# Moving the base blocks of 64x64 triangular inverses with two 256-column products in place of eight of 64 columns

## The chip, the cores and the metric

The kernel runs on one core of a Trainium2 chip. The metric is the device time of one execution in microseconds (us). TensorE is the matrix engine: PE stands for its products, PEld for its weight loads. VectorE is DVE, ScalarE is ACT, GpSimd is POOL.

## What is computed

Two transformer blocks, one behind the other, on 256 tokens of width 1024. The second one mixes tokens with two recurrences, a gated delta rule (GDN) and an RWKV-7 scan, both in chunks of 64 tokens and in two directions. Each chunk and head needs the solution of a unit lower triangular system of size 64. The kernel forms the inverse of that matrix; what is computed, cut to the part that matters, is

```python
CHUNK = 64
H_A, H_B = 4, 8                       # heads of GDN, of RWKV

def gated_delta_chunked(q, k, v, g, beta, s0):
    ...
    lower = jnp.where(strict, jnp.einsum('...id,...jd->...ij', k_beta, k) * decay, 0.0)
    a_mat = jnp.eye(CHUNK, dtype=jnp.float32) + lower
    rhs = jnp.concatenate([v * beta[..., None], k_beta * jnp.exp(gc)[..., None]], axis=-1)
    sol = lax.linalg.triangular_solve(a_mat, rhs, left_side=True, lower=True, unit_diagonal=True)
    ...

def rwkv7_scan(r, w, k, v, a, b, s0):
    def step(s, inp):
        r_t, w_t, k_t, v_t, a_t, b_t = inp
        sa = jnp.einsum('...vk,...k->...v', s, a_t)
        s = s * w_t[..., None, :] + sa[..., :, None] * b_t[..., None, :] + v_t[..., :, None] * k_t[..., None, :]
        return s, jnp.einsum('...vk,...k->...v', s, r_t)
    ...
```

The RWKV scan is computed in chunks of 64 too, so each of its chunks needs such an inverse as well.

## The kernel before

Each engine has its own in-order instruction stream; engines wait for each other on semaphores (`wait_ge`, `then_inc`). Up to about 1598 us the first block and the projections run. The GDN scan follows (about 1598 to 1712 us), then projections for RWKV, the RWKV scan (about 1830 to 2100 us), and the experts.

`Inverse64` (L1637) inverts eight 64x64 matrices at once. They lie as four blocks `c` side by side, in partitions 0 to 63 and again in 64 to 127; `HALVES` (L1622) gives for each half its own partitions and the other half's. The inverse is built by doubling: a base with blocks of size 2, then five levels. `TX[:, 0]` holds the inverse in one half order, `TX[:, 1]` its transpose in the other.

The base has four steps. POOL masks the matrices (`base_pool`, L1656), DVE adds the identity and so makes `Mb` (`base_dve`, L1662), PE moves it (`base_pe`, L1667), ACT copies both results from PSUM to SBUF (`base_act`, L1677, its instructions at L1682). `base_pe` fills two PSUM banks. `ps` gets each block transposed, in its own half: `Mb` is the stationary operand and the identity streams. `pt` gets each block as it is, in the other half: the identity is stationary and `Mb` streams. All of it goes through `mm` (L282). The mark `turned` follows the last product, and ACT waits for it before both copies.

The 64x64 products use a quarter of TensorE's array each. I call the quarters by rows and columns: A (rows 0 to 63, columns 0 to 63), B (rows 0 to 63, columns 64 to 127), C (rows 64 to 127, columns 0 to 63), D (rows 64 to 127, columns 64 to 127). A product reads its own half's partitions (its rows) and writes the partitions of its columns. So `ps` uses A and D, `pt` uses B and C, and the code before goes round A, B, D, C.

`mid_pe` (L1690) is the first product of a level and uses B and C; its right operand for level 1 is the ACT copy `inv_0`. `level_pe` (L1707) is the second product and uses all four quarters, except on the last level of RWKV.

The order of work is written by hand. `gdn_order` (L1738) lists pieces for four rounds, in each of which `base_b` runs `base_pe` for two inverses one behind the other. `rwkv_order` does the same for eight rounds. That makes 12 places with `base_pe` twice, 24 inverses, and 384 products of 64 columns. The list decides what PE does right behind them: in RWKV the piece `prep 0`, a 64x128 product and a one-row product of 512 columns each, and then `mid` of level 1; in GDN, by round, the `z` projection, `mid`, or products of the state.

An f32 product is issued as two weight loads and two products, and each of the two shows in the trace as a record of its own. So a 64-column f32 product is four instructions in PE's stream.

Of the kernel before, what the change touches and what calls it, by code (L numbers as in the profile page):

```python
# [32 lines left out]
C_I64, C_P64, C_Q64, C_L64 = 2690, 2754, 3010, 3138  # L33
# [54 lines left out]
class Counts:  # L88
# [13 lines left out]
    def did(self, name, *key, by=1):  # L102
        count = SHARED.get(name, name)
        self.n[count] = self.n.get(count, 0) + by
        self.value[(name, *key)] = self.n[count]
        return self.sem(name), by

    def at(self, name, *key):
        return self.sem(name), self.known[(name, *key)] if self.known else 1
# [112 lines left out]
def program(nc, A, out, known):  # L222
    stack = ExitStack()
    with stack:
# [22 lines left out]
        def bank(product, *readers, among=every_bank):  # L247

            n = bank_at.get(among, 0)
            b = among[n % len(among)]  # L250
            bank_at[among] = n + 1
            for mark in bank_free[b]:
                PE.wait_ge(*at(*mark))
            bank_free[b] = readers
            bank_of[product] = b
            return PS[b]
# [13 lines left out]
        def cst(col, n=128):  # L270
            return CST[:, col:col + n]
# [9 lines left out]
        def mm(o, lhsT, rhs, start, stop):  # L281
            return M.matmul(o, lhsT, rhs, start=start, stop=stop, skip_group_check=True)  # L282
# [1339 lines left out]
        HALVES = ((slice(0, 64), slice(64, 128)), (slice(64, 128), slice(0, 64)))  # L1622
# [14 lines left out]
        class Inverse64:  # L1637
# [29 lines left out]
            def base_pe(self, banks):  # L1667
                ps = bank(("turned", *self.tag), ("inv_own", *self.tag), among=banks)
                pt = bank(("turned_t", *self.tag), ("inv_0", *self.tag), among=banks)
                PE.wait_ge(*at("inv_t", *self.tag, 0))  # L1670
                for c in range(4):
                    for own, other in HALVES:
                        mm(ps[own, 64 * c:64 * c + 64], self.Mb[own, c, :], cst(C_I64, 64)[own, :], True, True)
                        ins = mm(pt[other, 64 * c:64 * c + 64], cst(C_I64, 64)[own, :], self.Mb[own, c, :], True, True)
                ins.then_inc(*did("turned", *self.tag))

            def base_act(self):  # L1677
# [2203 lines left out]
```

## Time and profile before

| | us |
|---|---|
| median of 3 runs | 2506.0 |
| lowest, highest | 2505.88, 2506.99 |
| the profiled execution | 2505.72 |
| its span in the trace | 2504.3 |

| engine | busy us | share of the span |
|---|---|---|
| PE | 2413.2 | 96% |
| PEld | 2085.4 | 83% |
| DVE | 1409.3 | 56% |
| ACT | 1193.5 | 48% |
| POOL | 294.3 | 12% |

PE's busy time counts any instant at which at least one product is under way. The sum over products that run beside each other in different quarters is larger. The granted clock was 0.993 of full speed on average.

### The profile page before, as it was taken

Reading aid. Unit: us, or ns where it says so; the run is one execution under the profiler, and the core shown is the slowest. Engines: PE = TensorE matmul, PEld = TensorE weight load, DVE = VectorE, ACT = ScalarE, POOL = GpSimd, SP = SyncE. Lnnn points to the kernel's source line nnn. Section 1 sums busy time; section 2 is a strip of 40 time slices with the busy share of each in tenths; the row PEclk is TensorE's granted clock in tenths of the full one; section 3 lists DMA queues with packets and bytes.
Section 4 is the critical chain, followed back from the end, with each engine's and each line's share of the span. In section 5 each row is a group of like instructions: output and inputs, shape, how many; then the busy total and the mean of one; then the engine's idle time right before and its main releaser. Section 6 shows DMA issues by size and latency. Waiting matters only on the chain.

```text
span 2504.3 us, 52401 instructions
## 1 busy us (share of the span) xinstructions
PE 2413.2 (96%) x23215; PEld 2085.4 (83%) x23215; DVE 1409.3 (56%) x2208; ACT 1193.5 (48%) x1725; POOL 294.3 (12%) x417
## 2 busy tenths in 40 slices
PE   7999999999999999999999999999999888999998
PEld 7999888799999998878899995687477777778787
DVE  5655544376646655533566557453534554378886
ACT  5434465544444434475454436431244442277775
POOL 0100000031101100000211000372123322000000
PEclk9999999999999999999999999999999999999999
DMA  8764522366656654413367522201111011479995
GB/s 256 244 211 152 203 83 92 116 202 202 227 194 202 216 203 160 167 70 119 127 204 255 194 97 101 69 4 40 68 36 37 24 50 41 134 250 365 368 362 183
DMA packets 269445, 396.15 MB, mean 158 GB/s; under 512 B 9624, under 2 KB 173133, under 8 KB 269085
## 3 DMA queue, kind: packets, MB, share of 16 engines
q1 hardware_dynamic: 267481, 389.32, 45.6%
q8 instruction: 185, 3.03, 0.5%
q0 software_dynamic: 1120, 2.17, 0.3%
q10 hardware_dynamic: 612, 1.24, 0.1%
q14 instruction: 47, 0.39, 0.1%
HBM read 391.66 MB, written 1.05 MB: 157 GB/s over the span
## 4 chain that ended last, share of the span: by engine, by line
PE 83%; DVE 6%; DMA 5%; ACT 3%; issue 2%; POOL 0%; SPq 0%; ACTq 0%; DVEq 0%; POOLq 0%
PE ps L282 82%; DMA RB<-in_moe_w_up 5%; DVE gwl L447 2%; ACT gwh L438 1%; DVE wl L447 0%; PE ps L1146 0%; ACT wh L438 0%; DVE AR L657 0%; ACT AR L2898 0%; DVE AT L1231 0%; DVE AR L1967 0%; PE ps L541 0%; ACT AR L2890 0%; ACT AT L1200 0%; DMA VR<-in_diff_gain 0%
## 5 line engine op out<-in xcount | busy, mean ns | idle before, releaser
L447 DVE TENSOR_TENSOR wl<-RB,wh 128x2048 fp32r<-128x2048 f32 (+5 forms) x189 | 412.5, 2186 | 284.8 <-ACT wh L438 284.3
L282 PE MATMUL ps<-H,RB 128*128 128x256 f32 (+2 forms) x1728 | 452.8, 421 | 2.8 <-ACT AR L2869 1.3
L438 ACT ACTIVATE wh<-RB 128x2048 fp32r<-128x2048 f32 (+5 forms) x189 | 342.2, 1815 | 232.6 <-PE ps L282 203.1
L282 PEld LDWEIGHTS ps<-H,RB 128*128 128x128 f32 (+1 forms) x1728 | 320.2, 189 | 114.9 <-issue 77.0
L282 PE MATMUL ps<-xhf,wl 128*128 128x256 f32 x1408 | 403.0, 286 | 3.7 <-DVE xlf L686 3.7
L282 PE MATMUL ps<-xlf,wh 128*128 128x256 f32 x1408 | 399.5, 284 | 0.0
L282 PE MATMUL ps<-xhf,wh 128*128 128x256 f32 x1408 | 399.4, 284 | 0.0
L282 PE MATMUL ps<-AR 64*64 64x64 f32 (+3 forms) x8296 | 258.3, 231 | 40.9 <-issue 24.0
L282 PEld LDWEIGHTS ps<-AR 64*64 64x64 f32 (+2 forms) x8296 | 225.1, 138 | 79.3 <-issue 64.3
L282 PEld LDWEIGHTS ps<-xhf,wl 128*128 128x128 f32 x1408 | 271.3, 193 | 14.2 <-issue 10.1
L282 PEld LDWEIGHTS ps<-xlf,wh 128*128 128x128 f32 x1408 | 271.4, 193 | 0.1
L282 PEld LDWEIGHTS ps<-xhf,wh 128*128 128x128 f32 x1408 | 271.3, 193 | 0.0
L447 DVE TENSOR_TENSOR gwl<-RB,gwh 128x2048 fp32r<-128x2048 f32 x96 | 217.2, 2289 | 37.2 <-ACT gwh L438 35.6
L438 ACT ACTIVATE gwh<-RB 128x2048 fp32r<-128x2048 f32 x96 | 183.2, 1926 | 44.2 <-DMA RB<-in_moe_w_up 30.1
L282 PE MATMUL ps<-hh,wl 128*128 128x256 f32 x704 | 199.2, 283 | 0.0
L282 PE MATMUL ps<-hl,wh 128*128 128x256 f32 x704 | 199.2, 283 | 0.0
L282 PE MATMUL ps<-hh,wh 128*128 128x256 f32 x704 | 199.2, 283 | 0.0
L791 ACT ACTIVATE H<-H 128x256 f32<-128x256 f32 x88 | 36.9, 419 | 294.7 <-DVE H L827 294.7
L282 PEld LDWEIGHTS ps<-hh,wl 128*128 128x128 f32 x704 | 135.2, 192 | 0.0
L282 PEld LDWEIGHTS ps<-hl,wh 128*128 128x128 f32 x704 | 135.2, 192 | 0.0
L282 PEld LDWEIGHTS ps<-hh,wh 128*128 128x128 f32 x704 | 135.2, 192 | 0.0
L1467 POOL TENSOR_TENSOR H<-H 128x256 f32<-128x256 f32 x48 | 45.6, 986 | 685.7 <-DVE H L1438 685.7
(445 smaller groups left out, 4105.3 us busy)
## 6 DMA issues: line engine op xcount, KB each, us to landing
RB<-in_ffn_w_gu SPq DMA_DIRECT2D x88, 1024.0 KB, 7.8
RB<-in_w_in SPq DMA_DIRECT2D x23, 2048.0 KB, 7.7
RB<-in_ffn_w_down SPq DMA_DIRECT2D x16, 2048.0 KB, 7.8
RB<-in_w_gate SPq DMA_DIRECT2D x16, 2048.0 KB, 8.7
RB<-in_moe_w_gate SPq DMA_DIRECT2D x32, 1024.0 KB, 7.6
RB<-in_moe_w_up SPq DMA_DIRECT2D x32, 1024.0 KB, 10.2
RB<-in_moe_w_down SPq DMA_DIRECT2D x32, 1024.0 KB, 8.0
RB<-in_ada_w SPq DMA_DIRECT2D x12, 2048.0 KB, 9.9
```

The source lines that it names most:

```text
L282: return M.matmul(o, lhsT, rhs, start=start, stop=stop, skip_group_check=True)
L438: S.activation(self.pair(h)[0], of(slot_of(*key)), ACT.Copy).then_inc(*did("high", *mark))
L447: V.tensor_tensor(lo, of(slot_of(*key)), hi.bitcast(F32), ALU.subtract).then_inc(*did("low", *mark))
L791: S.activation(sil[:, n % 4, 0, :], sil[:, n % 4, 0, :], ACT.Silu).then_inc(*did("silu", f, n))
L1467: P.tensor_tensor(HB[:, c, :], HB[:, c, :], tmp[:, (8 * i + c) % 4, :], ALU.add).then_inc(*did("merged", l, br, c))
```

## The change

In `base_pe` the loop over `c` now issues the products for `ps` alone, eight of 64 columns. Behind it come two products for `pt`, one for each half, that stream all four blocks (256 columns) through the identity. The mark `turned` is still on the last product. The values are the same.

```diff
                 for c in range(4):
-                    for own, other in HALVES:
+                    for own, _ in HALVES:
                         mm(ps[own, 64 * c:64 * c + 64], self.Mb[own, c, :], cst(C_I64, 64)[own, :], True, True)
-                        ins = mm(pt[other, 64 * c:64 * c + 64], cst(C_I64, 64)[own, :], self.Mb[own, c, :], True, True)
+
+                for own, other in HALVES:
+                    ins = mm(pt[other, 0:256].rearrange("p (c n) -> p c n", c=4), cst(C_I64, 64)[own, :], self.Mb[own],
+                             True, True)
                 ins.then_inc(*did("turned", *self.tag))
```

On PE, at the first place in the GDN scan (round 0): `ps<-CST,AR` is a product for `ps` (the constants stream), `ps<-AR,CST` one for `pt`. The rows ahead belong to the value rows, `ps<-RB,H` behind is the `z` projection.

```order
 L282 MATMUL ps<-RB,H 64x256 x32
 L282 MATMUL ps<-CST,AR_14745 64x128 x16
-L282 MATMUL ps<-CST,AR_14745 64x64
-L282 MATMUL ps<-AR_14745,CST 64x64
...
+L282 MATMUL ps<-CST,AR_14745 64x64 x8
+L282 MATMUL ps<-AR_14745,CST 64x256 x2
+L282 MATMUL ps<-CST,AR_14745 64x64 x8
+L282 MATMUL ps<-AR_14745,CST 64x256 x2
 L282 MATMUL ps<-RB,H 64x256 x16
```

What were 32 alternating products for the two inverses are now 8, 2, 8 and 2. Nothing else moved.

At the second place on PE (round 1 of GDN) the products of `mid`, which use B and C, stand right behind:

```order
 L282 MATMUL ps<-CST,AR_14745 64x64 x8
 L282 MATMUL ps<-AR_14745 64x64 x72
-L282 MATMUL ps<-CST,AR_14745 64x64
-L282 MATMUL ps<-AR_14745,CST 64x64
...
+L282 MATMUL ps<-AR_14745,CST 64x256 x2
+L282 MATMUL ps<-CST,AR_14745 64x64 x8
+L282 MATMUL ps<-AR_14745,CST 64x256 x2
 L282 MATMUL ps<-AR_14745 64x64 x16
```

There the last product for `pt` now stands next to `mid`, in the same quarters. DVE, ACT, POOL and SP keep their instructions and order.

## Rows read from the trace of the kernel before

**Rows 1.** The page's chain that ended last, shares of the span

```profile
PE 83%; DVE 6%; DMA 5%; ACT 3%; issue 2%; POOL 0%; SPq 0%; ACTq 0%; DVEq 0%; POOLq 0%
```

**Rows 2.** Chain of one RWKV round, 1860 to 1905: start, us, what

```profile
1859.99 1.88 PE ps L282 x82
1861.87 1.41 issue
1863.28 13.56 PE ps L282 x302
...
1880.15 7.17 PE ps L282 x253
1887.33 0.50 issue
1887.83 1.03 PE ps L282 x38
1888.87 0.12 issue
1888.99 1.97 PE ps L282 x85
1890.95 1.32 issue
1892.27 3.24 PE ps L282 x122
1895.51 0.50 issue
1896.01 9.00 PE ps L282 x144
```

**Rows 3.** PE groups by form, 1598 to 2110: busy us, mean ns, idle before, releaser

```profile
L282 PE MATMUL ps<-AR,CST 64*64 64x64 f32 x384 | 14.5, 222 | 0.0
```

**Rows 4.** Timeline of one place, RWKV round 1: start, us, what, xcount [idle before]

```profile
1870.00 0.27 PE L282 MATMUL ps<-CST,AR 64*64 64x64 f32 x1
...
1870.10 0.22 PE L282 MATMUL ps<-CST,AR 64*64 64x64 f32 x1
...
1870.16 0.22 PE L282 MATMUL ps<-CST,AR 64*64 64x64 f32 x1
...
1870.76 1.21 ACT L1682 ACTIVATE AR<-ps 128x256 f32<-128x256 f32 x4 [0.27 <-PE ps L282]
...
1870.92 0.22 PE L282 MATMUL ps<-CST,AR 64*64 64x64 f32 x1
1870.93 0.22 PE L282 MATMUL ps<-AR,CST 64*64 64x64 f32 x1
1870.93 0.22 PE L282 MATMUL ps<-CST,AR 64*64 64x64 f32 x1
1870.94 0.22 PE L282 MATMUL ps<-AR,CST 64*64 64x64 f32 x1
...
1871.09 1.12 PE L282 MATMUL ps<-H,AR 64*128 64x512 f32 x2
...
1872.14 1.12 PE L282 MATMUL ps<-H,CST 1*128 1x512 f32 x2
```

**Rows 5.** Timeline, a 256-column f32 product in two column halves at once

```profile
1604.14 1.90 PE L282 MATMUL ps<-RB,H 128*64 128x256 f32 x16
```

**Rows 6.** PE groups by form under way in 1958.30 to 1958.33

```profile
L282 PE MATMUL ps<-AR 64*64 64x64 f32 x9 | 0.5, 219 | 0.0
```

**Rows 7.** The same, 1958.335 to 1958.345, then 1958.56 to 1958.58

```profile
L282 PE MATMUL ps<-AR 64*64 64x64 f32 x8 | 0.4, 218 | 0.0
L282 PE MATMUL ps<-AR 64*64 64x128 f32 x2 | 0.3, 320 | 0.0
...
L282 PE MATMUL ps<-AR 64*64 64x128 f32 x4 | 0.4, 294 | 0.0
L282 PE MATMUL ps<-AR 64*64 64x64 f32 x6 | 0.3, 218 | 0.0
```

**Rows 8.** Timeline of GDN round 1, where the second inverse comes later

```profile
1629.66 0.27 PE L282 MATMUL ps<-CST,AR 64*64 64x64 f32 x1 [0.95 <-DVE AR L1664]
...
1630.14 0.22 PE L282 MATMUL ps<-AR,CST 64*64 64x64 f32 x1
1630.42 0.66 ACT L1682 ACTIVATE AR<-ps 128x256 f32<-128x256 f32 x2 [2.54 <-PE ps L282]
1630.50 0.24 PE L282 MATMUL ps<-CST,AR 64*64 64x64 f32 x1
...
1630.98 0.22 PE L282 MATMUL ps<-AR,CST 64*64 64x64 f32 x1
1631.18 1.12 PE L282 MATMUL ps<-AR 64*64 64x64 f32 x20
1631.26 0.66 ACT L1682 ACTIVATE AR<-ps 128x256 f32<-128x256 f32 x2 [0.17 <-PE ps L282]
```

**Rows 9.** Who PE waited for, 1598 to 2110: us in total, times, longest

```profile
PE ps L282 <- issue: 25.6, 24, 2.8
PE ps L282 <- POOL AR L1687: 5.8, 3, 2.2
PE ps L282 <- DVE AR L1664: 2.8, 4, 1.0
```

**Rows 10.** PE's timeline around three stalls of one round

```profile
2056.72 0.81 PE L282 MATMUL ps<-AR 64*64 64x64 f32 x40 [1.12 <-issue]
...
2060.69 2.14 PE L282 MATMUL ps<-AR 64*64 64x64 f32 x128 [0.92 <-issue]
2064.60 0.62 PE L282 MATMUL ps<-AR 64*64 64x64 f32 x25 [1.77 <-issue]
```

**Rows 11.** DMA queues of instructions: whole span, then 2060.68 to 2064.3 alone

```profile
q8 instruction: 185, 3.03, 0.5%
...
q8 instruction: 1, 0.02, 1.6%
```

**Rows 12.** Timeline of RWKV round 7, where `mid` follows the base directly

```profile
2074.69 0.22 PE L282 MATMUL ps<-AR,CST 64*64 64x64 f32 x1
2075.27 0.45 PE L282 MATMUL ps<-AR 64*64 64x64 f32 x14 [0.36 <-ACT AR L1682]
```

**Rows 13.** The scans' stretch: us, then busy us (x instructions) of each engine

```profile
1601.00:2110.00 509.00, 460.93 (x10570) 365.78 (x10566) 233.22 (x532) 186.45 (x446) 174.40 (x262) 0.99 0.12 37
```

## The prediction

> **What bounds the kernel.** I read the chain that ended last first: PE holds 83% of it, and no other engine more than 6% [rows 1]. In the scans, where the change lies, the chain is PE's own products, broken by pieces named "issue", in which PE waited for nothing that the profile shows [rows 2]. The waits of PE between 1598 and 2110 us say the same in sum: 25.6 us went to "issue" in 24 stalls, 5.8 us to POOL's masks and 2.8 us to the DVE step just ahead of the base [rows 9]. So time on PE counts nearly in full here, and there are two currencies: how long the array's quarters are held, and how many instructions PE's stream holds. The change costs in the first and saves in the second.
>
> The products that it removes are few. The 384 records for `pt` had PE busy 14.5 us in total [rows 3], and that time is not what can be gained, since nearly all of it lies beside the products for `ps`.
>
> **How the base runs now.** In RWKV round 1 the first record starts at 1870.00, the next ones at 1870.10 and 1870.16, the last four at 1870.92 to 1870.94 [rows 4]. Two inverses are 32 products, so 64 records, and these come as 16 groups of four, one record in each quarter. From 1870.10 to 1870.92 there are 14 steps in 0.82 us: 0.058 us a step. All quarters are free one step behind the last start, at 1870.98, so a place takes 0.98 us. The four quarters are full. The four products of `pt` in B are hidden behind the four of `ps` in A, and C behind D.
>
> **What a product of 256 columns takes.** The trace has none in a quarter of the array. The nearest is the `z` projection, 256 columns in two column halves at once: 16 records in 1.90 us, in eight steps, the last of which runs 0.38 us: (1.90 - 0.38) / 7 = 0.217 us a step [rows 5]. That is four times 0.058 less a small fixed part. A quarter with one such product is held 2 x 0.216 = 0.43 us. Before, four products of 64 columns held it 8 x 0.058 = 0.47 us. The bounds are 0.43 and, if a small fixed part came with each block, 0.47. I take 0.43. So B and C have no more work than before, and the question is only when they start it.
>
> **When B and C start.** Now eight products for A and D are issued first. In the last level of RWKV round 3, products of 64 columns are in B and C; behind them in the stream stand products of 128 columns for A and D. Up to 1958.33 records of 64 columns alone are under way [rows 6]; by 1958.345 two of 128 columns are under way too, and at 1958.56 six of 64 columns are, each lasting 0.22 us, so started after 1958.34 [rows 7]. Older narrow products thus start behind the first wide ones, three in each of their two quarters, with one just started in each. So a free quarter doesn't wait for the others to finish: its work starts when the busy ones have four records each left, and different widths run beside each other. I take that as the rule of this kernel's stream: each quarter holds two products, four records.
>
> The Trainium skill ("TensorE: Matmul & The Clock Gate", What overlaps and what doesn't) says that matmuls start and end strictly in program order. The rows above show later products starting ahead of older ones, so the measurement decides against that; what that rule would cost is the first rival below.
>
> **The sum for two inverses one behind the other.** Count from the first start. A and D run 16 steps as before and are free at 0.98. They have four records left of the first inverse when step 5 starts, at 0.10 + 3 x 0.058 = 0.27. B and C then start: 0.05 more for the first record of an idle quarter (0.10 against 0.058 between the first two starts, [rows 4]) and 0.43, so they are free at 0.75. The second inverse's A and D records have gone on meanwhile. Four are left at step 13, at 0.10 + 11 x 0.058 = 0.74; B and C go on at 0.75 and are free at 1.19. That is 0.21 us later than 0.98. Nine of the 12 places are of this kind (GDN rounds 0 and 2, RWKV rounds 1 to 7): 9 x 0.21 = 1.9 us.
>
> **For inverses that come apart.** In GDN round 1 the first runs from 1629.66 to 1630.14 and the second from 1630.50, because it waits for DVE [rows 8]; GDN round 3 and RWKV round 0 look the same. There the first is covered by the wait. The second took 0.10 + 7 x 0.058 = 0.51 us and takes 0.75: 0.24 later. Three places: 0.7 us.
>
> **Who feels it.** In RWKV rounds 0 to 6 the next product is of another tile shape, 64 rows by the full width. It starts at 1871.09, 0.15 us behind the last record's start [rows 4], so it waits for all quarters and starts later by what B and C take. ACT's copies start at 1870.76 and take 1.21 us, to 1871.97 [rows 4]. The first copy may start some 0.25 us later, which keeps the end at about 1872.2, and `mid` starts only behind the second 512-column product that began at 1872.14 and took 1.12 us: that delay is hidden. It would cost as soon as the copies ended more than 1 us later. In GDN round 1 and RWKV round 7 `mid` waits for these copies [rows 8, 12], so there the delay of `turned` is on the path, and it is the same 0.2 to 0.25 us, not another one. In GDN rounds 0, 2 and 3 other products follow and PE's end moves as in RWKV. Nothing runs free behind: the later waits for POOL and DVE hang on PE's own products. In all 1.9 + 0.7 = **2.6 us of cost**. From below the cost is bounded by nothing, if B and C start at the front of the stream in a way that no row shows; from above by the first rival.
>
> **What the shorter stream gives back.** The change removes six products for each inverse, 24 instructions, so 576 in all. The stalls on "issue" come in a rhythm: 2056.72, 2060.69, 2064.60 [rows 10]. Between the last two PE started 128 records, which with their weight loads are 256 instructions, and the queue that brings instructions moved one packet; over the span it moved 185 in 3.03 MB, 16 KB each, 256 instructions of 64 bytes [rows 10, 11]. So PE's stream comes in lines of 256, and where PE uses one up in less than some 3.9 us it waits for the next. The Trainium skill ("Advanced Engine Details and Errata", ISA Cache) says lines of 256 instructions too; the rows give the time. 576 instructions are 2.25 lines. Spread over all lines of the scans (10570 records and 10566 weight loads between 1601 and 2110 us, [rows 13], so 83 lines) the 25.6 us are 0.3 us a line and 2.25 lines give 0.7 us. If each saved line is one that stalls (24 stalls, 1.07 us each) they give 2.4 us. The base itself lies between long products, where lines don't stall, but its going shifts every later line end, in steps of 48 instructions a place, into other parts of the rounds. I take the middle, **1.5 us of gain**, and give the shift 3 us either way.
>
> **Sum.** 2.6 - 1.5 = +1.1 us against the profiled execution's 2505.7 us, which lies 0.3 us under the median of 2506.0. I put the difference on the median: 2507.1 us. What a measurement of this kernel can tell from no change is about 0.2%, 5 us.
>
> **Rivals.**
> 1. *The quarters don't overlap (slower).* If B and C start only behind the last record of A and D, and the next inverse's A and D only behind them, each inverse takes 8 x 0.058 + 0.43 us in place of 0.47. 24 x 0.43 = 10.4 us, less 1.5: +8.9, 2514.9 us. The skill's strict order would give nearly this. Against it stand [rows 6, 7]. It decides where the overlap of a wide and a narrow product falls under half of each. Chance 8%.
> 2. *The line ends fall badly (slower).* The 24 stalls last up to 2.8 us [rows 9]. If the shift adds five average stalls, 5 x 1.07 = 5.4 us, in place of the saving, the kernel takes 2.6 + 5.4 = +8.0, 2514.0 us. For it speaks that every round behind the first place gets other line ends; against it that there are fewer lines. Chance 6%.
> 3. *The stream is the bound (faster).* If lines, and not quarters, pace all of the scans, the wider products cost nothing and 2.25 lines of 3.9 us each are saved (from 2060.69 to 2064.60, [rows 10]): -8.8, 2497.2 us. Half of it, -4.4, would already show the base as covered. Against it: the base stands behind long products, and no stall is at its place in [rows 4]. Chance 6%.
>
> **How the numbers follow.** The forecast has 80%, with its own range of 2503 to 2511 us: the shift of 3 us either way, and 1 us for the cost. The whole range should leave out no more than 2 in 10; it reaches into the slower rivals, which hold more than the faster one: 2503 to 2513 us. Faster by over 0.2% (under 2501): part of rival 3 and a tail, 5%. Slower by over 0.2% (over 2511): rivals 1 and 2 and a tail, 14%. Within 0.2%: 81%.
>
> **What would show it in the trace after.** At each place 32 records of 64 columns and 8 of 256, the latter of about 0.38 us each and 0.216 us apart in one quarter. The first wide records start about 0.3 us behind the first narrow one, while narrow ones go on; if they start at 0.5 us, rival 1 holds. `prep 0` starts 1.3 us behind the base's first record, not 1.09. ACT's first copy starts about 0.25 us later. The stalls on "issue" stay about 24, at other places, with a sum of 21 to 28 us, and the instruction queue moves two or three packets fewer. I am wrong if the scans' stretch grows or shrinks by more than 4 us while those records look as I say, for then the stalls or a wait that I didn't see carry it.

## The result, and the profile after

The changed kernel takes **2512.97 us** (median of 20 runs, 2506.68 to 2516.46); the kernel before, timed in turn with it on the same chip, takes 2508.78 us (20 runs, 2503.91 to 2513.47). The ratio is **1.0019 (1.0013 to 1.0024)**. A second set of runs on another chip gave 1.0020 (1.0011 to 1.0029). So the change costs 4.8 us (0.5 us of standard error over both sets; means against means), where +1.1 us was forecast. That is still inside the 0.2% called "no change", and the time of 2512.97 us is inside the range, at its upper end. But the cost is certain, and it is four times the forecast. The profiled execution took 2510.31 us.

Who PE waited for from 1598 to 2115 us (us in total, times, longest), beside [rows 9]:

```profile
PE ps L282 <- issue: 26.3, 25, 2.6
PE ps L282 <- POOL AR L1690: 4.6, 3, 2.2
PE ps L282 <- DVE AR L1664: 2.4, 3, 1.1
```

The records of the 48 wide products, in PE's groups by form (busy us, mean ns, idle before), and the queue that brings instructions (packets, MB, share):

```profile
L282 PE MATMUL ps<-AR,CST 64*64 64x256 f32 x96 | 13.8, 398 | 0.0
...
q8 instruction: 183, 3.00, 0.5%
```

The 384 records of [rows 3] have become 96, nearly as busy as before (13.8 us against 14.5). Two packets fewer have come than in [rows 11], as forecast, but the stalls on "issue" did not shrink: 26.3 us in 25 against 25.6 in 24 (the prediction had 21 to 28 us in about 24).

The place of [rows 4], RWKV round 1, in the timeline after (start, us, engine, what, xcount, idle before):

```profile
1871.60 0.51 PE L282 MATMUL ps<-CST,AR 64*64 64x64 f32 x10
...
1871.89 0.43 PE L282 MATMUL ps<-AR,CST 64*64 64x256 f32 x2
1871.93 0.40 PE L282 MATMUL ps<-CST,AR 64*64 64x64 f32 x8
...
1872.16 0.38 PE L282 MATMUL ps<-AR,CST 64*64 64x256 f32 x2
...
1872.59 1.21 ACT L1685 ACTIVATE AR<-ps 128x256 f32<-128x256 f32 x4 [0.50 <-PE ps L282]
1872.62 0.38 PE L282 MATMUL ps<-AR,CST 64*64 64x256 f32 x2
...
1872.93 1.12 PE L282 MATMUL ps<-H,AR 64*128 64x512 f32 x2
```

Read it beside [rows 4]. The narrow records start at 1871.60 and the first wide ones 0.29 us behind, while narrow ones go on beside them. `prep 0` starts 1.34 us behind the first record where it started 1.09 us behind, so the place takes 0.25 us more. ACT's first copy starts 0.99 us behind the first record, before 0.76. All contiguous places but the one in RWKV round 7, where PE waits for ACT, show the same 1.34 us.

The next rows show something that the prediction had left out altogether. They are windows of RWKV round 1 after (us, then busy us and instructions of PE, PEld, DVE, ACT, POOL; the third figure from the end is the granted clock, 0.50 being 1.2 GHz):

```profile
1893.00:1894.00 1.00, 0.31 (x23) 0.17 (x11) 0.78 (x3) 0.00 (x0) 0.00 (x0) 1.00 0.00 0
1894.00:1895.00 1.00, 0.00 (x0) 0.00 (x0) 0.00 (x0) 0.00 (x0) 0.00 (x0) 1.00 0.00 0
1895.00:1896.00 1.00, 0.85 (x24) 0.85 (x28) 0.00 (x0) 0.38 (x1) 0.00 (x0) 0.65 0.00 0
1896.00:1897.00 1.00, 1.00 (x31) 1.00 (x29) 0.45 (x2) 0.00 (x0) 0.00 (x0) 0.50 0.07 16
...
1898.00:1899.00 1.00, 1.00 (x29) 1.00 (x28) 0.42 (x1) 0.98 (x2) 0.00 (x0) 0.64 0.00 0
1899.00:1900.00 1.00, 1.00 (x42) 1.00 (x39) 0.81 (x2) 0.56 (x1) 0.35 (x1) 1.00 0.00 0
```

The chain of the same stretch (start, us, what) tells what lies ahead of it:

```profile
1889.27 0.92 issue
...
1891.11 2.20 PE ps L282 x101
1893.31 1.84 issue
1895.15 4.86 PE ps L282 x120
```

PE waited 1.84 us for its stream. It went on at 1895.15, and 0.15 us later the clock fell to 1.2 GHz and stayed there for 3.4 us. At half speed 3.4 us do the work of 1.7. The same round before had its stalls of 1.32 and 0.50 us at other products ([rows 2], from 1890.95 on) and kept its clock at 1.00. The trace before has three such stretches in the scans (near 1620, 1651 and 1712 us), the trace after has three of the same kind (near 1626, 1653 and 1714 us) and the one above.

The stall does not decide this by itself. A second trace of the same changed kernel has the same stall at the same product, and no fall of the clock behind it (chain, then window):

```profile
1894.59 2.20 PE ps L282 x101
1896.79 1.56 issue
1898.35 5.70 PE ps L282 x154
...
1898.35:1904.05 5.70, 5.70 (x159) 5.50 (x160) 4.15 (x11) 2.43 (x4) 1.69 (x3) 1.00 0.02 6
```

So a stall can be followed by a slow stretch that costs as much again, but it need not be. Over the whole execution the clock does not tell the two profiled executions apart either: it is 0.993 in both, and they lie 4.6 us apart. From the start of the first place to that of the last the scans took 5.0 us longer after (477.4 against 472.4); 2.8 of that is in the eleven places between, and the one more stretch at 1.2 GHz is worth 1.7.

### The profile page after: what moved, and what is told of

It reads as the page before. It is cut to its first block, busy times and chain, and to the rows that moved or that the text cites. A ratio compares the mean times of both kernels' runs of the same rounds, so it can differ in the third digit from the quotient of the medians.

```text
span 2508.9 us, 51825 instructions
## 1 busy us (share of the span) xinstructions
PE 2419.5 (96%) x22927; PEld 2088.0 (83%) x22927; DVE 1409.3 (56%) x2208; ACT 1193.8 (48%) x1725; POOL 296.0 (12%) x417
## 4 chain that ended last, share of the span: by engine, by line
PE 82%; DVE 6%; DMA 5%; ACT 4%; issue 2%; POOL 0%; SPq 0%; ACTq 0%; DVEq 0%; POOLq 0%
PE ps L282 81%; DMA RB<-in_moe_w_up 4%; DVE gwl L447 2%; ACT gwh L438 1%; DMA RB<-in_moe_w_down 0%; DVE wl L447 0%; PE ps L1146 0%; ACT wh L438 0%; DVE AR L657 0%; ACT AR L2901 0%; DVE AT L1231 0%; DVE AR L1970 0%; PE ps L541 0%; ACT AR L2893 0%; ACT AT L1200 0%
```

## The experiments

None of the kernels leaves work out. "Mean" below is the mean of a kernel's runs less the mean of the runs of before in the same set, with one standard error, worked out from the single runs. "Clock" is the mean granted clock of the same runs, less before's. Over 2506 us, 0.001 of it is 2.5 us of TensorE's full-speed work lost, which is an upper figure for the time it costs, since a slower TensorE waits less for its stream. Each figure in that column has a standard error of 0.0003 to 0.0008, so most of them are not clear of nothing one by one.

| kernel | place, us | ratio (95%) | mean, us | clock |
|---|---|---|---|---|
| changed | 1.34 | 1.0019 (1.0013 to 1.0024) | +4.3 ± 0.8 | |
| changed, again | 1.34 | 1.0020 (1.0011 to 1.0029) | +5.4 ± 0.8 | -0.0006 |
| two loops, all of 64 columns | 1.49 | 1.0015 (1.0006 to 1.0024) | +3.6 ± 1.1 | -0.0002 |
| wide first | 1.09 | 1.0000 (0.9991 to 1.0009) | -0.2 ± 0.9 | -0.0009 |
| wide first, again | 1.09 | 1.0002 (0.9993 to 1.0011) | +0.9 ± 0.9 | -0.0012 |
| wide after two | 1.08 | 1.0000 (0.9991 to 1.0009) | 0.0 ± 0.7 | -0.0015 |
| wide first twice | 1.87 | 1.0016 (1.0006 to 1.0026) | +4.0 ± 0.9 | -0.0004 |
| GDN alone, wide first | 1.09 | 1.0007 (0.9998 to 1.0016) | +1.8 ± 1.0 | -0.0016 |
| GDN alone, as changed | 1.34 | 1.0018 (1.0008 to 1.0028) | +4.7 ± 1.2 | -0.0022 |
| RWKV alone, wide first | 1.09 | 0.9992 (0.9983 to 1.0001) | -2.0 ± 0.8 | +0.0003 |
| RWKV alone, wide first, again | 1.09 | 0.9995 (0.9983 to 1.0008) | -1.0 ± 1.3 | -0.0013 |
| RWKV alone, as changed | 1.34 | 1.0000 (0.9990 to 1.0011) | -0.4 ± 1.0 | +0.0004 |
| before, 64 wait instructions ahead | 1.09 | 1.0005 (0.9996 to 1.0014) | +1.3 ± 0.9 | -0.0007 |
| changed, filled with waits | 1.34 | 1.0150 (1.0136 to 1.0164) | +37.6 ± 0.7 | -0.0068 |

"Place" is a contiguous place, from its first product to the next other one.

**The order alone, in a stream of the old length.**

```diff
                 for c in range(4):
-                    for own, other in HALVES:
+                    for own, _ in HALVES:
                         mm(ps[own, 64 * c:64 * c + 64], self.Mb[own, c, :], cst(C_I64, 64)[own, :], True, True)
+                for c in range(4):
+                    for own, other in HALVES:
                         ins = mm(pt[other, 64 * c:64 * c + 64], cst(C_I64, 64)[own, :], self.Mb[own, c, :], True, True)
```

> The kernel before with the order of the change alone: the eight products for ps first, then the eight products of 64 columns for pt. Same instructions in number and length, so the stream's line ends stay where they were. Theory Q (the order costs: B and C start only once A and D have four records left, 0.27 us after the first start): a contiguous place is then 0.27 + 4 x 0.23 = 1.19 us in place of 0.98, +0.2 us at each of 12 places, +2.4 us in all, a ratio of 1.0010 (1.0006 to 1.0014). Rival S (the quarters cost nothing, and all that the change moved is where line ends fall): same as before, 1.0000 within 0.0004.

Slower by 3.6 us, with not one instruction more or less. The order costs, and rival S (only line ends count) falls. RWKV round 1 in its timeline:

```profile
1867.62 0.51 PE L282 MATMUL ps<-CST,AR 64*64 64x64 f32 x10
1867.92 0.27 PE L282 MATMUL ps<-AR,CST 64*64 64x64 f32 x2
...
1869.12 0.69 PE L282 MATMUL ps<-H,AR 64*128 64x512 f32 x1
```

B and C start 0.30 us behind A and D, as in the changed kernel. The place grew by 0.40 us, not 0.2. My working for it had forgotten that the stream is one. The likely reason for the rest is that the second inverse's products for A and D stand behind the later products of `pt` while these wait for room in B and C. The twelve places of this trace add up to 4.5 us more than before's, and 3.6 ± 1.1 were measured.

**The wide pair first.**

```diff
+                for own, other in HALVES:
+                    mm(pt[other, 0:256].rearrange("p (c n) -> p c n", c=4), cst(C_I64, 64)[own, :], self.Mb[own],
+                       True, True)
                 for c in range(4):
                     for own, _ in HALVES:
-                        mm(ps[own, 64 * c:64 * c + 64], self.Mb[own, c, :], cst(C_I64, 64)[own, :], True, True)
-
-                for own, other in HALVES:
-                    ins = mm(pt[other, 0:256].rearrange("p (c n) -> p c n", c=4), cst(C_I64, 64)[own, :], self.Mb[own],
-                             True, True)
+                        ins = mm(ps[own, 64 * c:64 * c + 64], self.Mb[own, c, :], cst(C_I64, 64)[own, :], True, True)
```

> The changed kernel with the two wide products ahead of the eight narrow ones. The stream is as short as the changed kernel's. Theory Q: all four quarters start at once (pt's two wide ones of 0.43 us lie in B and C while A and D take their four narrow ones of 0.22 us), so the place is 0.98 us again or a little less and the 3.0 us that the order cost are back; what is left over before is the shift of the line ends, +0.9 to +1.7 us: a ratio of 1.0003 to 1.0007, and about 3 us under the changed kernel. Rival S: no different from the changed kernel, 1.0019 (1.0013 to 1.0024).

> The kernel with the two wide products ahead of the eight narrow ones once more, word for word, beside the changed kernel. Theory Q (the order is what costs, 0.25 us at each of 12 places): 3.0 us under the changed kernel; the two measured so far stand 4.9 us apart, 1.3 us of uncertainty, over different chips. Theory G (the shorter stream is worth the 1.5 us of the prediction's sum): 0.9994 of before. Rival C (what the shorter stream gives in stalls is taken back by the granted clock: the first trace has six stretches at 1.2 GHz in the scans in place of three, each 3.4 us long and so worth 1.7 us): 1.0000 of before within 0.0004, with the mean clock 0.001 lower than before's.

Beside it, on the chip of the second set, ran the changed kernel:

> The changed kernel once more, word for word, beside its variants on one chip, so that they can be set against it directly; its trace tells whether the four stretches of 3.4 us at a granted clock of 1.2 GHz that the first trace has in the scans (at 1623, 1653, 1713 and 1893 us) belong to the program or to one execution. Theory Q: 1.0010 to 1.0024 of before, as measured before. Theory P (the stretches belong to the program): the same four places again; rival: others.

RWKV round 1 with the wide pair first:

```profile
1869.73 0.43 PE L282 MATMUL ps<-AR,CST 64*64 64x256 f32 x2
1869.74 0.45 PE L282 MATMUL ps<-CST,AR 64*64 64x64 f32 x8
...
1870.56 1.21 ACT L1684 ACTIVATE AR<-ps 128x256 f32<-128x256 f32 x4 [0.34 <-PE ps L282]
...
1870.82 1.12 PE L282 MATMUL ps<-H,AR 64*128 64x512 f32 x2
```

Wide and narrow start together, and the place is 1.09 us as in the kernel before. On one chip it stood 4.5 us (± 1.0) under the changed kernel, with the same number of instructions: theory Q holds in sign, and its 3.0 us lie 1.5 standard errors off. Theory G had 0.9994 for the shorter stream; 1.0000 and 1.0002 came. Each of the two intervals still holds 0.9994; all three sets of kernels with short places and the short stream together (+0.2 ± 0.5 us, next experiment) do not, and with them theory G falls. The clock was lower by 0.0009 ± 0.0005 and 0.0012 ± 0.0004, as rival C had it. The traces' stretches at 1.2 GHz belong partly to the program: both wide-first traces have one near 1620 or 1625 us and others near 1653, 1680, 1824 and 1841, and one more each, at 1997 and at 2026. The changed kernel's second trace, which runs 3 to 4 us later there, has those near 1629, 1657 and 1718 again, but not the one at 1895 shown above; it has two others, near 1684 and 2001.

**The wide pair behind two narrow products.**

```diff
                 for c in range(4):
                     for own, _ in HALVES:
-                        mm(ps[own, 64 * c:64 * c + 64], self.Mb[own, c, :], cst(C_I64, 64)[own, :], True, True)
+                        ins = mm(ps[own, 64 * c:64 * c + 64], self.Mb[own, c, :], cst(C_I64, 64)[own, :], True, True)
+                    for own, other in HALVES if c == 0 else ():
+                        mm(pt[other, 0:256].rearrange("p (c n) -> p c n", c=4), cst(C_I64, 64)[own, :], self.Mb[own],
+                           True, True)
```

> The two wide products behind the first two narrow ones, the other six narrow ones last: between the changed kernel (wide behind eight narrow ones) and wide-first. A look at the trace. Theory H (what costs is the head: narrow products ahead of the first wide one, during which pt's two quarters stand empty, and a wide one takes TensorE for 0.25 us wherever it lies): from a contiguous place's first product to the next other product 1.09 us plus 0.04 to 0.06 us, so 1.13 to 1.15 us; the changed kernel has 1.34. Rival (any narrow product ahead costs as much as all eight, since the start of both quarters is what counts): 1.3 us or more.

> The kernel with the wide pair behind the first two narrow products, word for word as looked at, now timed. Its places are 1.08 us in the trace, 0.26 us under the changed kernel's, with the same stream as wide-first. Theory Q: as wide-first, 1.0000 to 1.0003 of before, 3 to 4.5 us under the changed kernel. Rival (it was not the place but something else of wide-first that gained): 1.0010 or more.

The trace of the single execution of the first run:

```profile
1870.60 0.27 PE L282 MATMUL ps<-CST,AR 64*64 64x64 f32 x2
1870.62 0.43 PE L282 MATMUL ps<-AR,CST 64*64 64x256 f32 x2
1870.71 0.34 PE L282 MATMUL ps<-CST,AR 64*64 64x64 f32 x6
...
1871.68 0.69 PE L282 MATMUL ps<-H,AR 64*128 64x512 f32 x1
```

1.08 us from the first product to the next other one. Theory H (a narrow product ahead costs its own step, 1.13 to 1.15) and its rival both miss. One narrow product each in A and D leaves room, so the wide ones start 0.02 us behind. With four each in front they start 0.29 us behind. That fits the prediction's rule: two products, four records, for each quarter. Timed, it equals wide first. Over the three sets of kernels with short places and the short stream the mean is +0.2 ± 0.5 us; the changed kernel stands 4.6 ± 0.7 above them.

**The wide pair twice.**

```diff
-                for own, other in HALVES:
+                for own, other in 2 * HALVES:
                     mm(pt[other, 0:256].rearrange("p (c n) -> p c n", c=4), cst(C_I64, 64)[own, :], self.Mb[own],
```

> Wide-first with each pair of wide products issued twice (the second pair writes the same values again), 192 instructions more in the scans. Theory W (a wide product takes TensorE for 0.25 us even where its quarter is another than the last one's): a contiguous place grows from 1.09 to 2.1 us, each of the 12 places by 1.0 us, and if a place's time is paid one for one, 12 us over wide-first: 1.0048 of before. Rival Q2 (quarters work side by side, 0.43 us for a pair of wide ones): 1.73 us for the place, +0.64 each, 7.7 us: 1.0031. Rival X (a place's time is paid more than one for one, as 4.5 us for 12 x 0.25 us suggest): 18 us, 1.0072.

```profile
1871.99 0.43 PE L282 MATMUL ps<-AR,CST 64*64 64x256 f32 x2
...
1872.26 0.38 PE L282 MATMUL ps<-AR,CST 64*64 64x256 f32 x2
...
1873.33 0.38 PE L282 MATMUL ps<-AR,CST 64*64 64x256 f32 x2
...
1873.55 0.38 PE L282 MATMUL ps<-AR,CST 64*64 64x256 f32 x2
1873.86 1.12 PE L282 MATMUL ps<-H,AR 64*128 64x512 f32 x2
```

The wide records come two at a time, one in B and one in C, 0.22 us apart. Eight such steps from 1871.99 end at about 1873.75, 1.76 us: the quarters work side by side. Theory W would have 2.1 us. So the 0.43 us that the prediction gave a pair is right; my W had taken the starts' distance for the price of one product. The contiguous places grew by 0.78 us each (the others, which begin with a wait, by 0.4), 8.2 us over all 12, and the time by 3.8 ± 1.0 us over wide first (4.0 less 0.2). So a place's time is not paid one for one, and rival X falls too. One would think that the stream catches up while the array is held longer, but the trace does not show it: PE's stalls on "issue" in the scans are 25.3 us in 24, against 25.6 and 22.2 us in the two traces of wide first. Why only half is paid stays open.

**Each scan alone.** The new base applies only where a test of the inverse's tag holds ("r" for the RWKV scan, "g" for the GDN scan), and the other scan keeps the base of before:

```diff
+                if self.tag[0] == "r":
...
+                else:
                     for c in range(4):
                         for own, other in HALVES:
...
```

> The kernel before with wide-first bases in the four GDN places alone; the eight RWKV places keep the sixteen narrow products, so the RWKV scan's code is before's and only its line ends fall 192 instructions earlier. Theory G: 192 instructions are 0.75 of a line, worth -0.5 us; theory L (where line ends fall matters more than how many there are): off 1 by 1 us or more, in either direction; nothing at all: 1.0000 within 0.0004.

> The kernel before with wide-first bases in the eight RWKV places alone, where TensorE waits for its instruction stream most (23.5 of 26 us in the scans). The GDN scan is before's to the instruction. Theory G: 384 instructions fewer there are 1.5 lines, worth -1.0 us (-0.5 to -1.6): 0.9996; rival C: 1.0000 with a lower mean clock; rival L: 1 us or more in either direction by the line ends.

> The kernel with wide-first bases in the RWKV scan alone, word for word, a second time: at 0.9992 (0.9983 to 1.0001) it was the fastest so far, and its interval still held 1. Theory G (a shorter stream in the scan that waits for it is worth 1.5 to 2 us): 0.9992 to 0.9996 again, with a pooled interval under 1. Rival (chance): 1.0000 or above.

> The change in the RWKV scan alone (narrow ones first, then the wide pair), GDN as before. Its twin in the stream, wide-first in RWKV alone, stood at -1.7 us (0.7 us of uncertainty, two runs). Theory Q (0.25 us at each place, paid one for one): 8 x 0.25 = 2.0 us above the twin, so +0.3 us: 1.0001 of before. Rival X (paid at one and a half): 3.0 us above, +1.3 us: 1.0005. Rival R (the RWKV scan is where the whole changed kernel loses): +4.8 us, 1.0019.

> The change in the GDN scan alone, RWKV as before. Its twin, wide-first in GDN alone, stood at +1.8 us (1.0 us of uncertainty). Theory Q: 4 x 0.25 = 1.0 us above the twin, +2.8 us: 1.0011. Rival X: 1.5 us above, +3.3 us: 1.0013. Rival T (the twin's +1.8 was chance, and the GDN places cost their 1.0 us alone): 1.0004.

The order costs +1.2 ± 1.2 us in the eight RWKV places (-0.4 against the -1.7 ± 0.7 pooled of wide first there) and +2.9 ± 1.5 in the four GDN places. Expected were 2.0 and 1.0. Both lie within 1.3 standard errors, so these runs don't show more than 0.25 us a place. The shorter stream with short places gives **-1.7 ± 0.7 us** in RWKV alone, near the 1.0 that theory G asked for (its two runs gave -2.0 ± 0.8 and, repeated, -1.0 ± 1.3), and **+1.8 ± 1.0** in GDN alone. Together they are nothing, as wide first in both scans is; but of the four kernels' intervals here only that of the change in GDN alone leaves out 1. The change as it stands loses nothing in RWKV alone (1.0000) and shows its loss in GDN alone (1.0018). PE's stalls on "issue" from 1598 us to the scans' end, first in the trace with GDN alone changed, then in that with RWKV alone:

```profile
PE ps L282 <- issue: 25.4, 26, 2.6
```

```profile
PE ps L282 <- issue: 23.1, 21, 2.8
```

The windows of the two scans in the same order:

```profile
1598.00:2120.00 522.00, 476.55 (x10566) 377.80 (x10561) 235.31 (x538) 188.63 (x448) 176.71 (x266) 0.97 0.11 36
```

```profile
1598.00:2110.00 512.00, 467.58 (x10451) 369.41 (x10446) 234.68 (x535) 187.77 (x447) 175.29 (x264) 0.99 0.12 37
```

A granted clock of 0.97 against 0.99 over some 515 us is about 10 us of work lost, though this execution was one of the slower ones of its kernel (2513.7 us at a median of 2509.6). Over all runs the mean clock was 0.0022 ± 0.0006 lower than before's with GDN changed, and 0.0004 ± 0.0004 higher with RWKV changed. The table leans the same way: in the nine sets whose line ends in the RWKV scan are moved from its first place on, the clock was lower by 0.0004 to 0.0068; in the four where they start that scan as before, it differs by +0.0004, +0.0003, -0.0002 and -0.0013.

Where line ends fall does not fix it, though. In the two kernels with GDN alone changed (wide first, then as changed) the RWKV scan has before's code, and its line ends fall alike, since both save the same 192 instructions. From its first place to its last:

```profile
1839.90:2075.30 235.40, 213.45 (x6096) 183.21 (x6096) 113.52 (x267) 108.75 (x256) 73.90 (x101) 0.99 0.10 30
...
1840.60:2083.50 242.90, 218.79 (x6096) 186.51 (x6096) 113.58 (x267) 108.76 (x256) 73.56 (x101) 0.96 0.10 29
```

The same 6096 records took 235.4 us in one execution and 242.9 in the other, with 6.8 and 17.1 us at 1.2 GHz (5.1 us of work apart) and 13.9 and 17.9 us of stalls on "issue". So single executions differ by more here than any effect that is looked for, and that moved line ends bring the clock down is a lean of the means, not shown.

**Moving the line ends alone.**

```diff
+        def pad(n):
+            for _ in range(2 * n):
+                PE.engine.wait_ge(*at("x_in", 6))
...
             def conv_pe():
                 for n in range(13):
+                    if n in (1, 2):
+                        pad(32)
```

> The kernel before with 64 satisfied waits in TensorE's stream ahead of the GDN scan (32 in each of two convolution steps), so that every line end in both scans falls 64 instructions earlier in the work; nothing else differs. It tells how much the position of line ends is worth alone. Theory L (the sum's shift term was too small, the stalls at line ends differ by microseconds): moves by 1 us or more in either direction, a ratio off 1 by over 0.0004. Rival (the shift averages out over the 12 rounds): within 0.7 us, 0.9997 to 1.0003.

+1.3 ± 0.9: between the two theories, and undecided. `pad(n)` asks for 2n waits, and they come out as n instructions with two waits each: TensorE's queue has 636 wait instructions in this trace and 572 in before's. The waits are not free. They run from 1500.4 to 1507.2 us, one every 0.106 us, and where PE had no work left it stood still for 2.72 us; the clock fell behind that stall too, to 0.57 in the mean of 1504 to 1508 us. The first base starts 1.6 us later than before and the last one 0.5 us later. So in this one execution the scans took 1.1 us less, which is well inside what executions differ by. The trace shows how stalls and clock can trade: the stalls on "issue" in the scans fell from 25.6 us to

```profile
PE ps L282 <- issue: 19.0, 16, 2.5
```

and yet its span is 2505.4 us against 2504.3. It has eight stretches at 1.2 GHz in the scans, against three. The RWKV scan before, and with the line ends moved:

```profile
1837.27:2111.06 273.79, 240.52 (x7116) 206.43 (x7116) 123.09 (x293) 118.28 (x282) 86.88 (x125) 1.00 0.10 28
```

```profile
1838.00:2112.00 274.00, 245.13 (x7116) 212.27 (x7116) 123.45 (x293) 118.42 (x282) 87.45 (x125) 0.98 0.10 28
```

The same 7116 records, 274 us both times, 4.6 us more of them busy and less waited: the clock 0.02 lower took what the stalls gave. This is one pair of traces.

**The changed kernel, its stream filled up again.**

```diff
                     mm(ps[:, :], TW[u.rr, u.ts], W2[u.rr, :], True, False)
+                    if i > 0:
+                        pad(24)
```

(and the same behind the second product of `prep 0`, and four times `pad(48)` in the projections ahead of the RWKV scan)

> The changed kernel with waits that are already satisfied put into TensorE's stream so that, in the RWKV scan, line ends fall at the same products as in the kernel before: 48 in each of the eight RWKV rounds (24 between the two products of prep 0 and 24 behind them), and 480 over four steps of the projections ahead of that scan, of which 192 would make up for the GDN scan; the base is the changed one. Theory Q (order costs 0.25 us at each of 12 places): slower than before by 3 us plus what the waits themselves take, a ratio of 1.0012 or more. Rival S (line ends alone): with its line ends back in the RWKV scan it stands within 1 us of before, 1.0000 to 1.0005.

The expectation misstates two figures: the four steps hold 48 wait instructions each, 192 in all, not 480, and RWKV round 0 has none (`if i > 0`), so seven rounds have 48 and the whole is 528. The trace has them: 1100 wait instructions against 572. The experiment failed as a test, since the filling isn't free. The two products of `prep 0` in round 1 with 24 wait instructions between them:

```profile
1881.44 1.12 PE L282 MATMUL ps<-H,AR 64*128 64x512 f32 x2
1883.28 1.09 PE L282 MATMUL ps<-H,CST 1*128 1x512 f32 x2 [0.72 <-issue]
```

1.84 us apart, against 1.06 (1872.93 to 1873.99) in the changed kernel. The 24 instructions took longer than these 0.78 us: the trace has them from 1880.64 to 1883.17, one every 0.106 us, and the first ones run beside products that are still under way. PE's stalls from 1598 us to the scan's end, against 26.3 us in 25 in the changed kernel:

```profile
PE ps L282 <- issue: 45.3, 41, 2.3
```

The stops so cost 19.0 us. But 37.6 us were lost. The RWKV scan in this kernel:

```profile
1844.32:2148.24 303.92, 257.83 (x6923) 220.91 (x6924) 123.50 (x293) 118.65 (x282) 87.52 (x125) 0.94 0.09 25
```

A granted clock of 0.94 over 304 us is another 18 us; over all runs the clock was lower by 0.0068 ± 0.0004, 17 us. With small stops of TensorE put in by hand the clock came down, and that cost about as much again as the stops themselves.

## Why the prediction was off

- *The rule for the quarters, four records each*: right. Wide and narrow records run beside each other, the wide ones start 0.29 us behind the first narrow one (0.27 forecast), and with one narrow product in A and D ahead they start at once.
- *A pair of wide products in 0.43 us*: right. Steps of 0.22 us, B and C together, also with the pair doubled.
- *Cost of a contiguous place, 0.21 us*: 0.25 in the trace. The second record of the wide pair comes 0.27 us behind the first, not 0.22. The 12 places of the trace add up to 3.0 us, where the sum had 2.6. Measured in time, by the changed kernel against the three sets with short places and the same stream, the order costs 4.6 ± 0.7 us. So this term is 2.0 ± 0.7 short, and the places show only 0.4 of that.
- *ACT's copies and `mid` hidden*: right in RWKV rounds 0 to 6. In RWKV round 7 PE waits 0.34 us for ACT, before 0.36 [rows 12].
- *The stream gives 1.5 us back*: **the step that failed**, together with the size of the term above. With short places and the short stream the kernel was no faster than before (+0.2 ± 0.5 us over three sets). The term lay in the middle between an average line's share of one trace's stalls (0.7 us) and one whole stall for each saved line (2.4 us); neither bound, nor the shift of 3 us either way, was taken from a run in which line ends had moved. In the RWKV scan alone a gain is likely (-1.7 ± 0.7, where 1.0 of the 1.5 were its share). In the GDN scan alone the same edit comes to +1.8 ± 1.0, less than two standard errors from nothing. That it undoes the RWKV gain by moving the line ends would fit, and is not shown.
- *The granted clock*: not in the sum at all. The prediction counted stalls as the whole price of a line end. The trace shows a stall of 1.84 us with 3.4 us at 1.2 GHz behind it, and most kernels here with moved line ends ran at a lower mean clock. But the second trace has the stall without the fall, and the two profiled executions, 4.6 us apart, have the same mean clock of 0.993. That the clock is what the GDN change loses is argued from the means, not shown by an experiment that holds the clock.
- *Rivals*: 1 (no overlap) is out by the trace. 3 (the stream is the bound) is out: wide first gained nothing. 2 (the line ends fall badly) is out in its own form: there are not five more stalls but one (25 for 24), with 0.7 us more in them. That the same stalls at other products cost more by the clock is possible and open.

The account: 4.8 ± 0.5 us measured. 3.0 us are in the places. The stream's share is +0.2 ± 0.5 instead of -1.5. This leaves 1.6 us with an uncertainty of about 0.7. I can't place them. The doubled pair speaks against paying a place more than one for one; where the longer place moves the stalls and the clock behind it would be one explanation, and no run isolates that. Against the forecast of +1.1 the 3.7 us that were missing are 1.7 of the stream, 0.4 of the places and these 1.6. What is shown is that the order of the products costs, not the shorter stream: two kernels with the changed kernel's instructions in another order take 4.6 us less.

The experiments name a version: wide first, in the RWKV scan alone, at 0.9992 (0.9983 to 1.0001) and 0.9995 (0.9983 to 1.0008). Its pooled gain on the kernel before is 1.7 ± 0.7 us. It beats the changed kernel. That it beats the kernel before is likely but not certain: it was repeated because it had come out fastest, and the repeat alone gave 1.0 ± 1.3.

## What to carry to other kernels

When small products for different quarters of the array share one stream, order them so that the first product for each quarter comes before the second product for any other; one loop for the first pair of quarters and another for the second cost 0.25 to 0.40 us a place here, with the same values computed. Merging narrow products saves instructions, but count that gain only where the trace shows the stream to be waited for right there, and expect what lies behind to shift. Set such gains against the spread first: the profiled executions differed by up to 3.7 us in when the first base starts (1600.5 to 1604.2 us), ahead of all that was changed, and the same RWKV code took 235.4 and 242.9 us, so a term of 1 to 2 us can't be read from one pair of traces.

## What the runs showed of the hardware that I had not expected

- A stall at a line end of the instruction stream can be followed by 3.4 us at 1.2 GHz, 1.7 us more (1.84 us of stall in the first trace of the changed kernel); at the same product of the same kernel it can also pass without (1.56 us in the second trace). With 528 wait instructions put in, the clock took some 17 us on top of the stops' own 19.
- Fewer stalls need not mean less time: with 19.0 us of stalls over both scans in place of 25.6 the RWKV scan still took 274 us, at a clock of 0.98 in place of 1.00.
- An instruction that holds nothing but satisfied waits takes 0.106 us in TensorE's stream (24 of them from 1880.64 to 1883.17 us). Part of it is hidden beside products under way: 24 moved the next product by 0.78 us.
- Within one kernel the runs' time goes with their mean clock: the 35 runs of before in the second set differ by 0.9 us for 0.001 of clock (correlation -0.5), the 27 of the first set by 1.2 us (-0.8), the 23 and 29 of the other two by 1.5 and 0.8 us (-0.9 and -0.5). By the squares of these correlations the clock goes with a quarter of the runs' spread in two sets and with about 70% of it in the others (standard deviation 2.3 to 3.4 us).
